# Expert products: three rounded products per weight tile, or one native fp32 product on four column tiles

## The reference

```
aff = softmax(xt @ w_router)                       # per set: 512 latent, 128 context
g, idx = top_k(aff.T, cap)                         # cap = 64 latent, 16 context: 80 tokens an expert
xe  = xt[idx]
hid = silu(xe @ w_gate[e]) * (xe @ w_up[e])        # 1024 -> 2816, twice
ye  = (hid @ w_down[e]) * g                        # 2816 -> 1024
out = zeros.at[idx].add(ye)                        # 16 experts
```

## Time and profile before

| | us |
|---|---|
| median of 3 runs | 2213.56 (2211.67 to 2213.96) |
| the profiled execution, its own time | 2212.0 |
| its span in the trace | 2210.2 |
| mixture, first product to last result | 671.4 to 2180.4 |
| PE busy | 2117.9 (96%) |
| DVE busy | 1624.4 (73%) |
| ACT busy | 1388.4 (63%) |
| DMA, mean over the span | 288 GB/s |

### The profile page before, as it was taken

One profiled execution on the slowest core, in us unless ns is written; L12 is line 12 of the kernel. 1 busy time (PEld: TensorE's weight loads), 2 busy tenths in 40 slices (PEclk: granted clock), 3 DMA queues, 4 the chain that ended last, 5 costly groups with the idle time before them and its releaser, 6 DMA issues.

```text
span 2210.2 us, 30315 instructions
## 1 busy us (share of the span) xinstructions
PE 2117.9 (96%) x9431; PEld 1334.2 (60%) x9431; DVE 1624.4 (73%) x1967; ACT 1388.4 (63%) x1823; POOL 108.8 (5%) x133
## 2 busy tenths in 40 slices
PE   6999999999948999999999999999999999999994
PEld 3555555555745666666666666666666666666662
DVE  1220144424367999999999999999999999999995
ACT  3111134322226888788888888888888887888884
POOL 1000000000110000000000000000000000000002
PEclk9999999999968999999999999999999999999997
DMA  9531121002159999999999999999999999999962
GB/s 392 221 137 67 50 101 43 22 22 105 48 235 364 368 349 401 369 384 376 355 399 361 392 367 385 365 361 396 365 391 370 349 398 373 383 374 351 397 250 101
DMA packets 123362, 637.50 MB, mean 288 GB/s; under 512 B 12913, under 2 KB 21489, under 8 KB 75697
## 3 DMA queue, kind: packets, MB, share of 16 engines
q1 hardware_dynamic: 118560, 620.33, 70.8%
q0 software_dynamic: 4752, 16.52, 2.7%
HBM read 622.90 MB, written 13.89 MB: 288 GB/s over the span
## 4 chain that ended last, share of the span: by engine, by line
PE 92%; DVE 3%; DMA 2%; ACT 1%; issue 1%; POOL 0%; SPq 0%; POOLq 0%; ACTq 0%; DVEq 0%
PE ps L704 89%; DMA slab_x<-in_w_mod_blocks 1%; PE ps L1077 1%; DVE w_lo L1757 1%; ACT w_hi L1360 1%; PE ps L869 1%; PE ps L1096 0%; DMA xe<-xn_dram,idx_g 0%; PE ps L792 0%; DVE topi L1686 0%; PE ps L1000 0%; DVE topv L1685 0%; DMA ysum_dram<-yr,idx_s 0%; POOL rsx L617 0%; POOL rsx L618 0%
## 5 line engine op out<-in xcount | busy, mean ns | idle before, releaser
L1757 DVE TENSOR_TENSOR w_lo<-gu_ring,w_hi 128x1024 fp32r<-128x1024 f32 x704 | 853.0, 1221 | 67.6 <-ACT w_hi L1360 45.7
L1360 ACT ACTIVATE w_hi<-gu_ring 128x1024 fp32r<-128x1024 f32 x704 | 743.2, 1061 | 163.3 <-PE ps L704 159.2
L704 PE MATMUL ps<-w_hi,x_hi 128*80 128x512 f32 x1408 | 555.8, 395 | 5.9 <-DVE x_lo L1750 3.5
L704 PE MATMUL ps<-w_hi,x_lo 128*80 128x512 f32 x1408 | 553.4, 393 | 0.0
L1757 DVE TENSOR_TENSOR w_lo<-d_ring,w_hi 128x1024 fp32r<-128x1024 f32 x352 | 425.3, 1222 | 31.7 <-ACT w_hi L1360 17.3
L704 PE MATMUL ps<-w_lo,x_hi 128*80 128x512 f32 x1408 | 437.9, 392 | 1.7
L1360 ACT ACTIVATE w_hi<-d_ring 128x1024 fp32r<-128x1024 f32 x352 | 373.4, 1061 | 97.1 <-PE ps L704 94.5
L704 PEld LDWEIGHTS ps<-w_hi,x_hi 128*80 128x80 f32 x1408 | 208.7, 148 | 126.5 <-ACT w_hi L1360 10.5
L704 PE MATMUL ps<-w_hi,h_hi 128*80 128x512 f32 x704 | 283.0, 402 | 0.7 <-DVE h_lo L1770 0.7
L704 PEld LDWEIGHTS ps<-w_lo,x_hi 128*80 128x80 f32 x1408 | 206.8, 148 | 123.3 <-DVE w_lo L1757 9.8
L704 PE MATMUL ps<-w_hi,h_lo 128*80 128x512 f32 x704 | 276.7, 393 | 0.0
(11 more groups left out here) (188 smaller groups left out, 1474.6 us busy)
## 6 DMA issues: line engine op xcount, KB each, us to landing
gu_ring<-in_w_gu SPq DMA_DIRECT2D x352, 1024.0 KB, 8.7
d_ring<-in_w_down SPq DMA_DIRECT2D x352, 512.0 KB, 7.8
slab<-in_w_mod_blocks SPq DMA_DIRECT2D x7, 2048.0 KB, 12.4
slab<-in_w_in_blocks SPq DMA_DIRECT2D x6, 1536.0 KB, 8.9
gw<-in_w_gates SPq DMA_DIRECT2D x8, 1152.0 KB, 5.7
slab_y<-in_w_mod_blocks SPq DMA_DIRECT2D x4, 2048.0 KB, 12.8
x<-in_x_sample SPq DMA_DIRECT2D x8, 512.0 KB, 4.0
wo_sb<-in_w_out SPq DMA_DIRECT2D x1, 4096.0 KB, 12.7
```

The costliest lines, as they stand in the source:

```text
L704: return pe.matmul(out, lhsT, rhs, start=first, stop=last, **kw)
L1360: act.activation(unit_dst(w_hi, unit_slot(e, n)), unit_src(unit), ACT.Copy).then_inc(w_hi_ready, 1)
L1757: dve.tensor_tensor(unit_dst(w_lo, slot), unit_src(unit), unit_dst(w_hi, slot).bitcast(F32), ALU.subtract).then_inc(w_lo_ready, 1)
```

## The change

The split is gone: `high`, `low`, `tokens_high`, `tokens_low`, `h_high`, `h_low` and the tiles `w_hi`, `w_lo`, `x_hi`, `x_lo`, `h_hi`, `h_lo` are removed, and the products read the rings directly as native fp32. The 80 tokens are padded to 96 (16 zero columns) and taken as three thirds of 32. For each third, four products run on the four column tiles of the array, each with the same 32 tokens as the stationary operand and a different quarter of the weights' columns moving, and each into its own 32 partitions of one PSUM bank.

The FF width is done in three groups (`GW`: 4 x 256, 4 x 256, 4 x 192 columns). A gate/up chunk now holds one 128-row block of one group: 16 chunks of 1 MB and 8 of 0.75 MB (`w_gu_rest`). `silu` and `gated` work on 128 x 3 x 256 (or 192), three times an expert. In the down product two thirds share bank 3, with their two halves of the 1024 columns side by side, and the last third is in bank 4 with two chunks side by side, whose halves are summed in `result_sum`. The result is scattered as half rows of 512 by three indirect DMAs, and `ysum_dram` is [1280, 512]. Index and weight tables for these half rows are built once, by ten small VectorE instructions and five small transposes behind the top-k.

```diff
-GUR = 11
+GUR = 12
 DR = 11
+CP = 96
+NGRP = 3
+GW = (256, 256, 192)
+GD = (8, 8, 6)
...
+            def gate_up(e, G):
+                n = 2 * GW[G]
+                for k in range(KD):
+                    j = KD * G + k
+                    if k == 0 and G == 0:
+                        pe.wait_ge(x_add, val(e, 2, 2))
+                    if k == 0 and not (is_first(e) and G == 0):
+                        pe.wait_ge(hid_ready, val(e, NGRP, G))
+                    pe.wait_ge(gu_ld[j % GUR], val(e, 32, 16 * (j // GUR + 1)))
+                    for g in range(3):
+                        for x in range(4):
+                            last = mm(ps[32 * x:32 * x + 32, g, 0:n], xeT[:, k, 32 * g:32 * g + 32],
+                                      gu_ring[:, j % GUR, x * n:(x + 1) * n], k == 0, k == KD - 1)
+                    last.then_inc(gu_used, 1)
+                    if k == 0 and G > 0:
+                        hid_T(e, G - 1)
+                    elif k == 0 and not is_first(e):
+                        hid_T(before(e), NGRP - 1)
...
+                for g in range(3):
+                    last = pe.transpose(ps[:, 5, g * P:(g + 1) * P], hid[:, g, 0:P], ident)
+                for g in range(3):
+                    if G < 2:
+                        last = pe.transpose(ps[:, 6, g * P:(g + 1) * P], hid[:, g, P:2 * P], ident)
+                        continue
+                    for half in range(2):
+                        last = mm(ps[64 * half:64 * half + 64, 6, g * P:(g + 1) * P], hid[:, g, P:P + 64], ident, True, True)
...
+            def down(e, G):
+                pe.wait_ge(hidT_a, val(e, NGRP, G + 1))
+                pe.wait_ge(hidT_v, val(e, NGRP, G + 1))
+                if G == 0 and not is_first(e):
+                    pe.wait_ge(yr_ready, val(e, 2, 0))
+                for c in range(0, GD[G], 2):
+                    first, last_ = G == 0 and c == 0, G == 2 and c == GD[G] - 2
+                    w = [d_ring[(sum(GD[:G]) + c + i) % DR] for i in range(2)]
+                    for i in range(2):
+                        n_ = sum(GD[:G]) + c + i
+                        pe.wait_ge(d_ld[n_ % DR], val(e, 32, 16 * (n_ // DR + 1)))
+                        for x in range(4):
+                            mm(ps[32 * x:32 * x + 32, 3, :], inner(G, c + i, x % 2), w[i][:, x // 2 * 512:x // 2 * 512 + 512],
+                               first and i == 0, last_ and i == 1)
+                    for x in range(4):
+                        last = mm(ps[32 * x:32 * x + 32, 4, :], inner(G, c + x // 2, 2),
+                                  w[x // 2][:, x % 2 * 512:x % 2 * 512 + 512], first, last_)
+                    last.then_inc(d_used, 2)
+                    if G == 1 and c == 0 and not is_last(e):
+                        tokens_T(after(e))
...
+            def multiply_expert(e):
+                gate_up(e, 0)
+                if not is_first(e):
+                    down(before(e), 2)
+                gate_up(e, 1)
+                down(e, 0)
+                gate_up(e, 2)
+                down(e, 1)
...
+            def load_expert(e):
+                for j in range(8):
+                    gu_load(e, j)
+                for c in range(16, 22):
+                    d_load(before(e), c)
+                for j in range(8, 16):
+                    gu_load(e, j)
+                for c in range(8):
+                    d_load(e, c)
+                for j in range(16, 24):
+                    gu_load(e, j)
+                for c in range(8, 16):
+                    d_load(e, c)
...
+            def silu(e, G):
+                act.wait_ge(gu_used, val(e, 24, KD * (G + 1)))
+                if G > 0 or not is_first(e):
+                    act.wait_ge(hid_ready, val(e, NGRP, G))
+                act.activation(sil[:, :, 0:GW[G]], ps[:, 0:3, 0:GW[G]], ACT.Silu).then_inc(sil_ready, 1)
...
+            def gated(e, G):
...
+                dve.tensor_tensor(hid[:, :, 0:n], sil[:, :, 0:n], ps[:, 0:3, n:2 * n], ALU.mult).then_inc(hid_ready, 1)
...
+            def result_sum(e):
+                dve.wait_ge(d_used, val(e, NF, NF))
+                dve.tensor_copy(yb[:, :], ps[64:128, 4, :]).then_inc(yb_high, 1)
+                dve.wait_ge(yb_high, val(e, 1, 1))
+                dve.wait_ge(yb_low, val(e, 1, 1))
+                dve.scalar_tensor_tensor(yrB[0:64, :], yb[:, :], gB[:, bass.ds(number(e), 1)], yrB[0:64, :],
+                                         ALU.mult, ALU.add).then_inc(yr_ready, 1)
...
             def scatter():
-                pool.indirect_dma_start(ysum_dram[:, :], bass.IndirectOffsetOnAxis(ap=idx_s[:, :], axis=0),
-                                        yr[:, :], None, compute_op=ALU.add).then_inc(scattered, 16)
+                for idx, rows in ((idx_sA[:, :], yrA[:, :]), (idx_sB[0][:, :], yrB[0:CC, :]),
+                                  (idx_sB[1][:, :], yrB[32:32 + CC, :])):
+                    pool.indirect_dma_start(ysum_dram[:, :], bass.IndirectOffsetOnAxis(ap=idx, axis=0), rows, None,
+                                            compute_op=ALU.add).then_inc(scattered, 16)
```

More of the change, by code:

```diff
@@ L442, in is_first, with is_last, before, after @@
             return isinstance(e[0], int) and number(e) == 0
[L444 to L468, removed]
+        def is_last(e):
+            return isinstance(e[0], int) and number(e) == E_ - 1
+        def before(e):
+            return (e[0], e[1] - 1)
+        def after(e):
+            return (e[0], e[1] + 1)
         def loaded(eng, kind, i):
@@ L548, in gu_load @@
                 if j >= GUR:
[L549 to L556, removed]
@@ L571, in load_expert @@
-            def load_expert(e):
[L573 to L583, removed]
+                    sp.wait_ge(gu_used, val(e, 24, j - GUR + 1))
+                elif not is_first(e):
+                    sp.wait_ge(gu_used, val(before(e), 24, j + GUR + 1))
@@ L1060, in gate_up @@
-            def gate_up(e, s, q):
-                if q == 0 and s >= 3:
-                    pe.wait_ge(hid_ready, val(e, NS, s - 2))
-                elif q == 0 and not is_first(e):
-                    pe.wait_ge(hid_ready, val(e, NS, (s + 9 if s < 2 else 8) - NS + 1))
-                split_product(e, place["gu", s, q], lambda a_: ps[0:CT, s % 3, :],
-                              lambda a_: (x_hi[:, 2 * q + a_, :], x_lo[:, 2 * q + a_, :]),
-                              lambda a_: q == 0 and a_ == 0, lambda a_: q == KD // 2 - 1 and a_ == 1)
@@ L1071, in hid_T @@
-            def hid_T(e, s):
-                pe.wait_ge(hid_ready, val(e, NS, s + 1))
-                if s >= 1 or not is_first(e):
-                    pe.wait_ge(hT_lo_ready, val(e, NS, s))
-                for f in range(2):
-                    last = pe.transpose(ps[:, 7, f * CT:(f + 1) * CT], hid[:, f * P:(f + 1) * P], par[0:CT, 0:CT])
-                last.then_inc(hidT_done, 1)
-            def down(e, s, f, at_):
-                if f == 0:
-                    pe.wait_ge(hT_lo_ready, val(e, NS, s + 1))
-                if s == 0 and f == 0:
-                    pe.wait_ge(yr_ready, val(e, 1, 1))
-                split_product(at_, place["d", s, f], lambda a_: ps[0:CT, 5 + a_, :],
-                              lambda a_: (h_hi[s % 3][:, f, :], h_lo[s % 3][:, f, :]),
-                              lambda a_: s == 0 and f == 0, lambda a_: s == NS - 1 and f == 1)
+            pe.transpose(ps[0:CT, 5, 0:E_], topf[:, :], par[0:E_, 0:E_]).then_inc(topT_done, 1)
@@ L1098, in tokens_T @@
                 last.then_inc(xeT_done, 1)
-            def before(e):
-                return (e[0], e[1] - 1)
-            def after(e):
-                return (e[0], e[1] + 1)
-            def multiply_expert(e, more):
-                for s in range(NS):
-                    for q in range(KD // 2):
-                        if s == 0 and q == 0:
-                            pe.wait_ge(xeT_ev, val(e, 1, 1))
-                        gate_up(e, s, q)
-                        if s == NS - 1 and q == 1:
-                            hid_T(e, s - 1)
-                    if s == 0 and not is_first(e):
-                        hid_T(before(e), NS - 1)
-                    if 1 <= s < NS - 1:
-                        hid_T(e, s - 1)
-                    if s == 3 and more:
-                        tokens_T(after(e))
-                    if s == 1 and not is_first(e):
-                        for f in range(2):
-                            down(before(e), NS - 1, f, e)
-                    if s >= 2:
-                        for f in range(2):
-                            down(e, s - 2, f, e)
-                for f in range(2):
-                    down(e, NS - 2, f, e)
+            def multiply_expert(e):
[6 more added lines that the diff above has]
+                down(e, 1)
@@ L1130, in _ @@
             tokens_T((0, 0))
-            multiply_expert((0, 0), True)
+            multiply_expert((0, 0))
             with pe.Fori(0, E_ - 2) as r:
```

(43 more changed lines are left out.)

367 lines of the change are left out of this document (145 added, 222 removed).

## The result

The changed kernel takes 2223.4 us (median of 6 runs, 2221.97 to 2224.32), the kernel before, measured beside it, 2213.41 (2210.89 to 2214.46). The ratio is 1.0047, 95% interval 1.0034 to 1.0060: it is slower by 10 us. I had forecast 2150, faster by 63. The time lies in the stated range, and the sign is that of a rival.

The account below looks back on a forecast made before the run. TensorE's products were taken as the bound, transfers some 7% behind. Turns of 89.9 instead of 93.88 us bring the mixture from 1509 to 1442 us; -67 + 4 = -63 gives 2149, or 2150 beside the median; range 2128 to 2240.

Parts of the forecast that it names:

- the sign is that of a rival: Whole kernel: faster by over 0.2% had chance 0.75, within 0.2% 0.03, slower 0.22.
- the sum's silent term for the jump back: TensorE's loop over experts: the sum counted no time for jumping back, taking the repeated code as not fetched again.
- The loop is fetched anew: TensorE's loop: each of 13 jumps back waits up to 8.7 us for code; 2150 to 2263, middle 2205; chance 0.13.
- Products: Gate/up and down on column tiles: quads 0.43 and 0.3225 us apart, 85.1 us an expert in place of 91.3.
- Transposes and changes of tiling: TensorE's turn: transposes with the 64-column products 3.9 us, switches between tiles and whole array 0.9 us an expert.
- Transfers: Weight loads: floor of 87.4 us a turn, 2.5 below TensorE; as the pace, 2165 to 2190 us, chance 0.17.
- Covers: Work beside TensorE: `silu`, `gated`, copies and in-loop scatters stay hidden; without `down` as cover, 7 us an expert.
- Instruction pace: TensorE's 384-column groups: a 54 ns floor per instruction gives 2251 us, deciding from 48 ns on; chance 0.13.
- Start: Before the first product: gather 1.6 us later, token split of 1.65 us gone, zero in sum.
- End: Behind the last expert: copy, scaled copy and sum, then two more scatter issues of 2.9 us; plus 4 us.
- at its ends: Mixture beyond its 16 turns: 4 us kept of 7, for first products at a lower clock and last copies.

Follow-up runs that it names:

- slot 0: Changed kernel with the first instruction of TensorE's loop on the start of a block of 256 instructions, no hint: 2138.86 us, ratio 0.9670.
- slot 128: Changed kernel with the first instruction of TensorE's loop in the middle of a block of 256 instructions; no hint: 2223.71 us, with the hint: 2138.55 us.
- the kernel written out: Changed kernel with TensorE's loop over the 14 middle experts written out, the other engines keeping their loops: 2138.87 us, ratio 0.9672.
- the hinted kernel: Changed kernel with `hint_back_edge=True` at TensorE's loop, not placed on a chosen slot: 2138.07 us, ratio 0.9661.
- the light load: Changed kernel, loop kept, with loads from the second expert on bringing a third of the bytes and products run in full: 2192.57 us, one run.

## Why the prediction was wrong

**The step that failed** is the sum's silent term for the jump back: nothing, on the strength of a body that the kernel before does not fetch again. That row holds for a body of 948 instructions (852, 84 of the loop and its registers, 12 waits), and I carried it to a body of nearly twice the length. The term measured 6.4 us a jump, 95.56 - 89.15; 13 of them are 83 us, and 2223.4 - 2138.9 = 84.5 is what the kernel gains with the jump written out. That is more than the whole miss of 73, since the rest of the sum was 11 too high.

**The rival was named, with the right mechanism, and given 0.13.** "The loop is fetched anew" had up to 8.7 us a jump, its middle 2205; 4.67 of pause and 1.7 of slow clock were measured. That 2223.4 lies in the stated range is owed to this rival; the step that made 2150 the likeliest was wrong. The prediction puts against it that no row shows such a wait; the slow clock was not in its price. In the runs a plain loop keeps 7 blocks (42 packets at slot 0) and not 8 (159 at slot 128). 1771 instructions fit in seven blocks from 22 of 256 starting slots, so a loop that lies anywhere misses 11 times in 12. With the limit of 7, which only the runs gave, the rival's chance would have been near 0.9; without it, a body of 1750 instructions, where the rows show only one of 852 that is not fetched again, still was reason for more than 0.13, and the range of 2150 to 2263 had the answer in it.

**The other terms**, as the kernel written out shows them:

- Products: 85.1 us an expert. The quads are 0.43 and 0.32 us apart over the whole mixture. Right. A product on the whole array with 384 columns moving takes 0.3225 us a record, and here four records, one on each column tile, take 0.32 together, so four go in the time of one.
- Transposes and changes of tiling: 3.9 + 0.9 = 4.8 us summed, 89.15 - 85.1 = 4.0 measured in the kernel written out. The 64-column products do run in pairs there: 12 records in 0.81 us (1025.65 to 1026.46 in its timeline), where 1.4 were summed. Over 16 experts the 0.75 is 12 us, about what 2138.9 lies below 2150.
- Transfers: floor of 87.4 us a turn summed, 86.3 measured; they did not become the pace. Right.
- Covers: `silu`, `gated`, the copies and the scatters were hidden in the loop. One cover was missed: in the first expert no `down` stands between `gate_up(0)` and `gate_up(1)`, and TensorE waits for `hid`:

```profile
695.67 2.78 PE L692 MATMUL ps<-gu_ring,xeT 128*32 128x512 f32 x24 [3.27 <-DVE hid L1714]
```

  ScalarE's part of it includes 1.28 us of a table load before the first `silu`. In the hinted kernel the granted clock fell to 0.50 behind the same wait, and the same 24 records took 5.34 us.
- Instruction pace: the rival's threshold was off by a little. With 48 quads of 384 columns an expert, a floor takes the gain of 4.0 us back from some 51 ns an instruction on, and not from 48. The measured 40 ns make it idle.
- Start: zero summed; the first product comes at 670.07 instead of 671.35. End: 4 us summed. In the kernel written out 33.8 us lie between the last product and the end of the span, against 29.9 before: right. Between them the mixture takes 1432.4 us, 16 x 89.15 and 6 at its ends, where 4 were summed. (The lower clock in that term: in the kernel before the granted clock was 0.50 from 671 to 677 us, behind the wait for the tokens.)

Had the jump been free, the sum would have been 11 us too high, 63 of gain forecast and 74 had.

**What remains open.** Where the limit lies exactly: counted from the start of the loop's first block, 1771 instructions stay and 1893 and 1899 don't, and that it is the 1792 of seven whole blocks is the likeliest reading and was not tried. Why seven is open too, and so is how the hint keeps a body that touches eight: no run shows it. What the 3.1 us of a pause under the light load consist of is open as well, and so is why the clock falls behind some pauses of 3.1 us and not behind others.

## What to carry to other kernels

Count the instructions of every loop body when products get smaller and more numerous, the register operations and the waits too (a native fp32 product is four instructions), and compare it in whole blocks with what stays resident (here 7 blocks of 256 did, and 8 did not without the hint); a change that is right in every engine's arithmetic can lose all of it, here 85 us, at the jump. Look at the queue of instruction packets on the page of before and after: it pointed at the cause in one line, 31 and 158. A hint for the jump, or the loop's head on a block's start, cost one line of code and gives the best versions here, 2138.1 and 2138.9 us, 3.3% under the kernel before; writing out the loop gives the same.

## What the runs showed of the hardware

- Two programs with the same instructions in the same order, with TensorE's loop at slot 0 or at slot 128 of a block, take 2138.9 and 2223.7 us.
- With the hint (`hint_back_edge=True`) a body that touches 8 blocks is not fetched again (42 and 35 packets), while without it all of it is, and more: 159 packets less 42, over 13 jumps, and 89 less 35, over 6, are both 9 a turn.
- In the changed kernel each of the 13 pauses of 4.5 to 4.9 us was followed by slow records (24 in 4.3 to 5.3 us instead of 2.76; the granted clock was 0.64 and 0.76 behind the one at 1036.68 us); under the light load pauses of 2.4 to 3.9 us were followed by slow records (4.5 to 5.4 us) in five cases of eleven.
- Four column tiles with native fp32 products sustain one quad per 0.43 us (512 columns) or 0.32 us (384 columns) over a whole mixture, beside 395 GB/s of transfers, with TensorE busy 1215 of 1215 us.
